# The first product of two MLPs with stationary weights, tokens' high and low parts side by side

## The reference

```
y = _rms_norm(h, mlp_norm_g[layer])
h = h + jnp.square(jax.nn.relu(y @ w_up[layer])) @ w_down[layer]
```

## Time and profile before

| | |
|---|---|
| median of 3 runs | 1504.51 us (1504.07 to 1504.88) |
| profiled execution, its own time | 1503.38 us |
| its span in the trace | 1501.6 us |
| TensorE busy | 1473.5 us, 98% |
| VectorE busy | 1040.9 us, 69% |
| ScalarE busy | 701.8 us, 47% |
| chain that ended last | 93% TensorE, 4% VectorE, 2% ScalarE |

### The profile page before, as it was taken

The page is one execution under the profiler, slowest core; times in us unless marked ns, Lnnn a source line. Parts: engine busy times, 40 slices in busy tenths (PEclk is TensorE's granted clock), DMA queues, the critical chain, the costliest instruction groups (busy, mean ns, idle before and its releaser), DMA issues.

```text
span 1501.6 us, 17885 instructions
## 1 busy us (share of the span) xinstructions
PE 1473.5 (98%) x7310; PEld 1225.6 (82%) x7310; DVE 1040.9 (69%) x1205; ACT 701.8 (47%) x882; POOL 32.3 (2%) x63
## 2 busy tenths in 40 slices
PE   8999999999999999999999999999999999999997
PEld 6788888898688888788887788887888889888886
DVE  5778676766687767778887788776554567665554
ACT  6364544534764444634444534445433453454432
POOL 1000000000000000100000000000000000000000
PEclk9999999999999999999999999999999999999999
DMA  8477877787478788588884588866555555555662
GB/s 310 144 247 278 305 275 257 247 285 239 127 255 291 265 285 297 188 302 291 311 276 131 185 307 304 298 231 215 183 185 179 187 177 169 169 181 185 195 190 76
DMA packets 202285, 346.22 MB, mean 231 GB/s; under 512 B 9643, under 2 KB 105139, under 8 KB 202204
## 3 DMA queue, kind: packets, MB, share of 16 engines
q1 hardware_dynamic: 163836, 269.45, 54.0%
q10 hardware_dynamic: 38368, 75.64, 14.0%
HBM read 343.96 MB, written 1.09 MB: 230 GB/s over the span
## 4 chain that ended last, share of the span: by engine, by line
PE 93%; DVE 4%; ACT 2%; issue 1%; POOL 0%; DMA 0%; DVEq 0%; POOLq 0%; ACTq 0%
PE up_ps L1535 57%; PE acc L1535 32%; PE tr_ps L1649 3%; PE tr_ps L1778 1%; PE tr_ps L1881 1%; DVE res L1142 1%; ACT w_hi L587 0%; DVE w_lo L1004 0%; DVE xn L1139 0%; ACT xn L632 0%; ACT xn L617 0%; DVE xT_lo L1053 0%; DMA res<-in_x 0%; POOL msq L554 0%; POOL rstd L548 0%
## 5 line engine op out<-in xcount | busy, mean ns | idle before, releaser
L1004 DVE TENSOR_TENSOR w_lo<-raw,w_hi 128x2048 fp32r<-128x2048 f32 x238 | 540.5, 2291 | 199.9 <-ACT w_hi L587 199.7
L587 ACT ACTIVATE w_hi<-raw 128x2048 fp32r<-128x2048 f32 x243 | 457.8, 1916 | 65.8 <-DVE ada_acc L1100 35.9
L1535 PE MATMUL up_ps<-w_hi,xT_hi 128*128 128x512 f32 x1120 | 448.1, 400 | 5.9 <-DVE xT_lo L1053 2.8
L1535 PE MATMUL up_ps<-w_hi,xT_lo 128*128 128x512 f32 x1120 | 438.3, 391 | 0.0
L1535 PE MATMUL up_ps<-w_lo,xT_hi 128*128 128x512 f32 x1120 | 437.6, 391 | 0.0
L1535 PEld LDWEIGHTS up_ps<-w_hi,xT_hi 128*128 128x128 f32 x1120 | 211.0, 188 | 55.1 <-issue 7.8
L1535 PEld LDWEIGHTS up_ps<-w_hi,xT_lo 128*128 128x128 f32 x1120 | 210.9, 188 | 45.6
L1535 PEld LDWEIGHTS up_ps<-w_lo,xT_hi 128*128 128x128 f32 x1120 | 211.4, 189 | 40.5
L1535 PE MATMUL acc<-w_hi,hT_hi 128*128 128x512 f32 x656 | 209.0, 392 | 0.3 <-DVE hT_lo L1033 0.3
L1535 PE MATMUL acc<-w_hi,hT_lo 128*128 128x512 f32 x656 | 207.2, 390 | 0.0
L1535 PE MATMUL acc<-w_lo,hT_hi 128*128 128x512 f32 x656 | 207.1, 390 | 0.0
(11 more groups left out here) (155 smaller groups left out, 982.8 us busy)
## 6 DMA issues: line engine op xcount, KB each, us to landing
raw<-in_ffn_w_in SPq DMA_DIRECT2D x176, 512.0 KB, 4.9
ada_raw<-in_ada_w ACTq DMA_DIRECT2D x72, 1024.0 KB, 7.5
raw<-in_ffn_w_out SPq DMA_DIRECT2D x88, 512.0 KB, 4.6
raw<-in_w_up SPq DMA_DIRECT2D x64, 512.0 KB, 5.5
raw<-in_w_down SPq DMA_DIRECT2D x64, 512.0 KB, 4.5
raw<-in_b_w_qkv SPq DMA_DIRECT2D x36, 512.0 KB, 4.7
raw<-in_conv_w_in SPq DMA_DIRECT2D x24, 512.0 KB, 4.4
raw<-in_a_w_in SPq DMA_DIRECT2D x16, 512.0 KB, 8.3
```

Source lines behind the costliest of these rows:

```text
L587: nc.scalar.activation(w_hi[:, slot, :], raw[:, slot, :], ACT.Copy).then_inc(hi_ready, 1)
L1004: nc.vector.tensor_tensor(w_lo[:, slot, :], raw[:, slot, :], w_hi[:, slot, :].bitcast(F32), ALU.subtract).then_inc(lo_ready, 1)
L1535: return nc.tensor.matmul(dst, a, b, start=start, stop=stop, skip_group_check=True)
```

## The change

In chunks 1 to 7 of both MLPs the roles in the first product are swapped. `wide_block` takes a 128 x 128 tile of the weights as stationary operand. With `w_hi` it moves 512 columns: the 256 tokens' high parts and their 256 low parts, which lie in one tensor `xT` now. With `w_lo` it moves the 256 high parts alone. Both go into one bank: its left half sums high x high and low x high, its right half high x low. The result has hidden units on its partitions, so nothing is transposed afterwards. A chunk has four such blocks, and these take four banks, the two of `up_ps` (hidden units 0 to 255) and the two of `tr_ps` (256 to 511).

Afterwards ScalarE copies the right halves to `pre` (`low_half`), VectorE adds the left halves (`low_add`), ScalarE applies ReLU and squares into `mid` (`squared`) and rounds to `hT_hi` (`squared_hi`), and VectorE subtracts (`squared_lo`). `squared_hi` waits until the second product of the chunk before has used that half of `hT_hi`. Chunk 0 stays as it was, with its transposes.

```diff
-        xT_hi = sb("xT_hi", [P, KT, TOKENS], F32R)
-        xT_lo = sb("xT_lo", [P, KT, TOKENS], F32R)
+        xT = sb("xT", [P, 2, KT, TOKENS], F32R)
+        xT_hi, xT_lo = xT[:, 0, :, :], xT[:, 1, :, :]
...
+        def wide_banks(h):
+
+            return (up_ps, tr_ps)[h][:, :, :]
```

In ScalarE's part of the MLP:

```diff
                 def step(c, g):
                     load_ada(unit0 + c, 0)
                     ahead(g)
                     if c > 1:
                         load_ada(unit0 + c, 1)
-                    for t in range(TT):
-                        hidden(c, t, g)
+                    for h in range(2):
+                        low_half(c, h, g)
                     if c == 1:
 
                         load_ada(unit0 + c, 1)
+                    for h in range(2):
+                        squared(c, h)
                     ahead(g + 1)
                     ahead(g + 2)
-                    transposed(c)
+                    for h in range(2):
+                        squared_hi(c, h, g)
                     ahead(g + 3)
```

In VectorE's:

```diff
                 def step(c, g):
-                    for s in range(2):
-                        ahead(g + s)
-                        ada(unit0 + c, s)
-                        if s == 0:
-                            mod_sums(name, c)
+                    ahead(g)
+                    ada(unit0 + c, 0)
+                    for h in range(2):
+                        low_add(c, h)
+                    ada(unit0 + c, 1)
+                    ahead(g + 1)
                     ahead(g + 2)
-                    transposed(c)
+                    squared_lo(c, 0)
+                    if c + 1 < MLP_CHUNKS:
+                        mod_sums(name, c + 1)
+                    squared_lo(c, 1)
                     ahead(g + 3)
```

In TensorE's:

```diff
+            def wide_block(g, s, n):
+
+                slot = (g + s) % RING
+                dst = wide_banks(n // 2)[:, n % 2, :]
+                for i in range(UPK):
+                    k = s * UPK + i
+                    cols = slice(i * UPN + n * P, i * UPN + (n + 1) * P)
+                    mm(dst.rearrange("p (h n) -> p h n", h=2), w_hi[:, slot, cols], xT[:, :, k, :], start=(k == 0))
+                    last = mm(dst[:, 0:TOKENS], w_lo[:, slot, cols], xT_hi[:, k, :], stop=(k == KT - 1))
+                return last
...
+                def hidden_block(c, gb, s, n):
+
+                    if n == 0:
+                        pe.wait_ge(lo_ready, gb + s + 1)
+                    if s == 0 and n % 2 == 0:
+                        if n:
+                            pe.wait_ge(tr_read, mid_fill(p, name, c))
+                        elif c > 1:
+                            pe.wait_ge(low_added, wide_pair(m0, c - 1, 0) // 2 + 1)
+                    if (c, s) == (1, 0) and n < 2:
+                        pe.wait_ge(relu_done, 2 * m0 + n + 1)
+                    last = wide_block(gb, s, n)
...
+                def wide_chunk(c, gb):
+
+                    if c == 1:
+                        for s in range(2):
+                            for n in range(2):
+                                hidden_block(c, gb, s, n)
+                            if s == 0:
+                                for t in range(TT):
+                                    turn_mid(0, t)
+                        for s in range(2):
+                            for n in range(2, 4):
+                                hidden_block(c, gb, s, n)
+                        return
+                    for s in range(2):
+                        for n in range(4):
+                            hidden_block(c, gb, s, n)
...
-                for c in range(1, MLP_CHUNKS - 1):
+                for c in range(1, MLP_CHUNKS):
                     gb = g + 4 * c - 2
-                    up_chunk(gb, (relu_done, 2 * (m0 + c - 1) + 1), lambda s, t: between(c, s, t))
-                    for s in range(2):
-                        down_slab(gb + 2 + s, hT_hi, hT_lo, 2 * s, c == 1 and s == 0,
-                                  (mid_fill(p, name, c - 1), 1))
-                    for t in range(TT):
-                        turn_mid(c, t)
...
+                    wide_chunk(c, gb)
+                    down_part(c - 1, gb + 2, 0)
+                    if c + 1 < MLP_CHUNKS:
+                        modulation(name, c + 1)
+                    down_part(c - 1, gb + 2, 1)
```

More of the change, by code:

```diff
@@ L300, in build @@
         gelu_done, relu_done, mlp_mid = sem("gelu_done"), sem("relu_done"), sem("mlp_mid")
+        low_copied, low_added, wide_lo = sem("low_copied"), sem("low_added"), sem("wide_lo")
         var_ready, ln_rstd, vn_ready, mix_ready, gated = (sem("var_ready"), sem("ln_rstd"), sem("vn_ready"),
@@ L371, in block_of, with wide_pair @@
             return up_ps[:, n // 2, (n % 2) * TOKENS:(n % 2 + 1) * TOKENS]
+        def wide_banks(h):
+            return (up_ps, tr_ps)[h][:, :, :]
+        def wide_pair(m0, c, h):
+            return 2 * (m0 // MLP_CHUNKS * (MLP_CHUNKS - 1) + c - 1) + h
         def flipped_pair(h):
@@ L1239, in mlp @@
                 p = at[name]
+                m0 = 0 if name == "mlp0" else MLP_CHUNKS
                 unit0 = ADA_AT[name]
@@ L1620, in down_slab, with down_last @@
                 last.then_inc(slab_used, 1)
-            def down_last(g, hi, lo, k0, start, ready=None, between=None):
+            def down_last(g, hi, lo, k0, start, ready=None, between=None, second=None):
                 for t in range(TT):
@@ L1634, in down_last @@
                         pe.wait_ge(lo_ready, g + 2)
+                        if second is not None:
+                            second()
                     last = down_halves(g + 1, t, hi, lo, k0 + 2, between if t else None)
@@ L1801, in turn_mid @@
                     turn(mid, t, 0, 4, mid_fill(p, name, c) + t)
-                def between(c, s, t):
-                    if (c, s, t) == (1, 0, 0):
-                        for t in range(TT):
-                            turn_mid(0, t)
-                    elif (s, t) == (0, 1):
-                        modulation(name, c)
+                def hidden_block(c, gb, s, n):
[9 more added lines that the diff above has]
+                    last = wide_block(gb, s, n)
+                    if (s, n) == (1, 1):
+                        last.then_inc(up0_ready, 1)
+                    elif (s, n) == (1, 2):
+                        last.then_inc(tr_ready, TT)
+                    elif n == 3:
+                        last.then_inc(slab_used, 1)
@@ L1810, in mlp, with down_part @@
+                def down_part(c, gd, s):
+                    if c == 0:
+                        down_slab(gd + s, hT_hi, hT_lo, 2 * s, s == 0, (mid_fill(p, name, 0), 1))
+                    else:
+                        pe.wait_ge(wide_lo, wide_pair(m0, c, s) + 1)
+                        down_slab(gd + s, hT_hi, hT_lo, 2 * s, False)
                 first_chunk(name)
-                for c in range(1, MLP_CHUNKS - 1):
+                for c in range(1, MLP_CHUNKS):
                     gb = g + 4 * c - 2
-                    up_chunk(gb, (relu_done, 2 * (m0 + c - 1) + 1), lambda s, t: between(c, s, t))
-                    for s in range(2):
-                        down_slab(gb + 2 + s, hT_hi, hT_lo, 2 * s, c == 1 and s == 0,
-                                  (mid_fill(p, name, c - 1), 1))
-                    for t in range(TT):
-                        turn_mid(c, t)
@@ L1820, in mlp @@
[L1820 to L1829, removed]
-                          (lambda: turn_norm(after, 0)) if early else None)
+                    wide_chunk(c, gb)
@@ new lines, in mlp, with second_pair @@
+                    down_part(c - 1, gb + 2, 0)
+                    if c + 1 < MLP_CHUNKS:
+                        modulation(name, c + 1)
+                    down_part(c - 1, gb + 2, 1)
+                def second_pair():
+                    pe.wait_ge(wide_lo, wide_pair(m0, MLP_CHUNKS - 1, 1) + 1)
+                pe.wait_ge(wide_lo, wide_pair(m0, MLP_CHUNKS - 1, 0) + 1)
+                down_last(gb + 4, hT_hi, hT_lo, 0, False, between=(lambda: turn_norm(after, 0)) if early else None,
+                          second=second_pair)
```

37 lines of the change are left out of this document (added).

## The result

The changed kernel took 1509.24 us in the median of six runs (1508.39 to 1510.53), the kernel before 1504.52 us in six runs (1502.89 to 1505.86). The medians lie 4.7 us apart, a ratio of 1.0031; the ratio estimated over all runs is 1.0038, with a 95% interval of 1.0028 to 1.0048: slower by 4 to 7 us. The forecast was 1502.1 with a range to 1509.0.

The account below looks back on a forecast made before the run. TensorE was taken to bound the kernel. Per MLP, -4.9 us saved plus stalls of 1.85 and 1.8 made -1.2, both MLPs -2.4 us: 1502.1 against the median 1504.51, range 1498 to 1509.

Parts of the forecast that it names:

- what bounds the kernel: Whole kernel: TensorE, busy 98% of the span; in the MLP the chain holds nothing but its pieces.
- both waits: Per MLP, TensorE stalls 1.85 us in chunk 1 for tr_ps and 1.8 us before chunk 2 for w_lo.
- The last chunk, where 0.7 us of margin was reckoned: Last chunk of each MLP: hT_lo wanted at 22.0, with 0.7 us left, so no stall.
- what the transposes are worth: After each of chunks 1 to 7, eight transposes removed: 0.90 us a chunk.
- I take 0.347: First product: a 512-column plus a 256-column matmul cost 0.347 us; 32 pairs make 11.10 us a chunk.
- slower by a dearer pair: Rival, 448 pairs: two-place operand or size change costs something; at 15 ns a pair +6.7 us, 1508.8; chance 0.12.
- where the forecast had -1.2: Per MLP: -4.9 us saved, plus stalls of 1.85 and 1.8 us, about -1.2 us.
- A clock that falls at the gaps: Sign that the forecast is wrong: TensorE's clock falling at its gaps; no size given.
- the rule of the Trainium skill's page: Weight loads overlap only into another row group; 16 more a chunk would cost 1.7 us, some 24 in 14 chunks.
- 32 x 0.415: First product, rival of weights that show: a pair at 0.415 us, +30.5 us in all, 1532.6; chance 0.04.

Follow-up runs that it names:

- the first layout test: Changed kernel with the tokens' high and low parts interleaved by contraction tile, so the 512 columns are one run: 1510.16 us, ratio 1.0043.
- the grouped kernel with its gaps: Changed kernel, both waits kept, with four matmuls of 512 columns and then four of 256 in place of alternating: 1510.92 us, ratio 1.0045.
- the two ungrouped ones with neither wait: Changed kernel with both reorderings on VectorE: 1499.45 us; and that kernel with three matmuls of 256 columns per weight tile: 1502.78 us.
- one filled kernel: Changed kernel with useless matmuls ahead of both waits, the second piece ahead of chunk 0's second down slab: 1508.52 us, ratio 1.0031.
- the other has more work: Changed kernel with useless matmuls ahead of the first wait, but the second piece misplaced behind the second gap: 1515.99 us, ratio 1.0077.
- that of three matmuls of 256 columns: Kernel without the two waits, with the 512-column matmul undone into two of 256, three per weight tile: 1502.78 us, ratio 0.9994.

## Why the prediction was wrong

**Right: what bounds the kernel, and both waits.** The first was forecast at 1.85 us, released by `hT_lo`, and is 1.8; the second at 1.8, released by `w_lo` behind the modulation load, and is 2.2, since the load took 7.7 us to its use and not 7.04. They are at their places in both MLPs and nowhere else in them, and taking away either or both confirmed them. The last chunk, where 0.7 us of margin was reckoned, has no wait.

**Right: what the transposes are worth,** 0.90 us a chunk. With all waits gone the period is 0.45 us under that of before, and the two products themselves account for the rest.

**Wrong: "I take 0.347" for the pair.** Starts alternate by 0.236 and 0.117, in sum 0.353. A chunk's first product is 163.25 - 151.96 = 11.29 us and not 11.10, so that, with 0.06 more in the second product (10.94), the saving is 0.45 a chunk and not 0.70: 14 x 0.25 = 3.5 us. The cost is one of changing between 512 and 256 columns. A first product takes 11.29 us with sixteen changes in eight pairs, 11.20 with four, 11.15 with two, and 32 x 0.347 = 11.10 would be the sum with none. It isn't one price per change (the last two changes taken away saved 0.05, the twelve before them 0.09), and what makes it up stays open. The rival "slower by a dearer pair" named the mechanism, at 5 ns a pair to lose the gain; it was 6 ns. Why the second product takes 0.06 more isn't known either.

**Mis-sized besides:** the second wait by 0.4 us, and the restart behind each wait, which the sum had at nothing. The 32 matmuls behind the first wait take 5.93 us, where they take 5.67 in the kernel without that wait; the sixteen behind the second take 3.09 in place of 2.81. In all, the first MLP's own rows give 7 x (22.23 - 22.68) + 1.8 + 2.2 + 0.26 + 0.28 = +1.4 us, and 1.27 was measured, where the forecast had -1.2.

**Left out of the sum: the clock.** "A clock that falls at the gaps" stood among the signs of a wrong prediction and had no price. A half-clock stretch costs 1.5 to 1.6 us here (7.41 - 5.93, 4.57 - 3.09, 7.40 - 5.82). The traces of the six kernels that kept a gap of about 2 us or more in the MLPs have 18 such gaps, and 8 of them have a stretch behind them: one in the changed kernel, three in the first layout test, three in the grouped kernel with its gaps, one in the kernel without the second wait. In the MLPs of all 13 traces no stretch stands anywhere else. Nor is it the change alone: every trace, that of before too, has the same gap of 2.12 us once more, behind the MLPs, and in 9 of the 13 a stretch begins within 2 us of its end. By 8 of 18, an estimate, four new gaps cost 4 x 8/18 x 1.5 = 2.7 us on the average.

**The sum, then:** 3.5 from the pair and the second product, 0.8 from the second wait less 0.1 from the first, 1.1 from the four restarts: 5.3. The clock adds 3.0 in the profiled pair, and some 2 by the mean clocks (0.0018 to 0.0025 less than before, at 0.9 us per 0.001): 7.3 to 8.3 in all. The forecast and the measured median lie 7.1 us apart, by the ratio 8.1. The last part is the least certain. That idle TensorE brings such stretches rests on where they stand. The mean clocks bear it out in part. Against before on the same chip, the layout test and the grouped kernel, with both waits, lie 0.0029 and 0.0045 lower; but the two kernels with one wait lie 0.0010 and 0.0012 lower, and the two ungrouped ones with neither wait 0.0013. Filling the gaps doesn't settle it: one filled kernel is 1 us faster than the change, within its interval, and the other has more work and a lower clock. Whether the stretch in the attention has to do with the change isn't shown: of the traces without a gap of 2 us in the MLPs, that of three matmuls of 256 columns and that of the filled kernel have it, and before's and the others have not.

**On weight loads,** the rule of the Trainium skill's page "TensorE: Matmul & The Clock Gate", section "Part 3: Packing small matmuls — row/col tiling", would have had them show at full row groups. The traces do not agree: 24 loads in a row before matmuls of 256 columns leave a step of 0.120 us, as the earlier trace rows had it, and the 11.29 us of a first product are far from 32 x 0.415 = 13.3.

## What to carry to other kernels

A change that shortens a loop's steady period by 2% can be lost in its first two turns: list what each bank and each queue entry is released by in turns 0 to 2, and move the instruction that nobody waits for behind the one that TensorE waits for. Here two such moves turned +0.4% into -0.3%. A price "in between" two measured forms (here 512 and 256 columns in turn) is an unknown with a range of its own, multiplied by the count, and grouping equal shapes is the cheap test. And a new gap on TensorE should be priced with the restart (0.3 us here) and the clock behind it, not as its idle time alone.

## What the hardware showed that was not expected

Alternating between matmuls of 512 and 256 columns costs 6 ns a pair over the two sizes by themselves, and grouping by eight gives back about three quarters of it (11.29, 11.15 and 11.10 us a chunk).

A gap of 1.7 to 2.5 us on TensorE in the MLPs was followed in 8 of 17 cases by a stretch at 1.2 GHz that cost 1.5 to 1.6 us, nearly as much as the gap; one gap of 3.2 us had none. One and the same gap of 2.12 us, in all 13 kernels, had such a stretch behind it in 9.

An operand of 512 columns in two pieces, 2,048 elements apart, moves as fast as one in a single piece (period 22.23 in both, and 22.13 in both once grouped by four).
